# Expert weights of one fused layer kernel: the down matrices move from SyncE's DMA queue to ScalarE's

## The reference

```
logits = hf @ w_router + b_router             # 256 tokens, 32 experts, top 4 kept
gu  = xb @ w_gate_up[e] + b_gate_up[e]        # [rows,1024] @ [1024,2048]
g   = min(gu[:, :1024], 7);  u = clip(gu[:, 1024:], -7, 7)
y   = ((u + 1) * g * sigmoid(1.702 * g)) @ w_down[e] + b_down[e]   # [rows,1024] @ [1024,1024]
x  += weighted sum of y over the four experts of each token
```

## Time and profile before

| what | value |
|---|---|
| median of three runs | 1425.66 us |
| the profiled execution | 1425.22 us |
| its span | 1423.0 us |
| PE busy | 1337.5 us (94%) |
| ACT busy | 316.1 us (22%) |
| DVE busy | 479.2 us (34%) |
| DMA, whole span | 498.75 MB, mean 351 GB/s |

### The profile page before, as it was taken

The page is one execution under the profiler, slowest core; times in us unless marked ns, Lnnn a source line. Parts: engine busy times, 40 slices in busy tenths (PEclk is TensorE's granted clock), DMA queues, the critical chain, the costliest instruction groups (busy, mean ns, idle before and its releaser), DMA issues.

```text
span 1423.0 us, 16623 instructions
## 1 busy us (share of the span) xinstructions
PE 1337.5 (94%) x6794; PEld 712.5 (50%) x6794; DVE 479.2 (34%) x696; ACT 316.1 (22%) x416; POOL 36.2 (3%) x50
## 2 busy tenths in 40 slices
PE   8989999999999999999899999898999989999998
PEld 5758866334334333333333333333333336897996
DVE  3676665112112111211121111211112116775764
ACT  4254633011111110110111101111011114632531
POOL 2110100000000000000000000000000000000000
PEclk9999999999999999999999999999999999999999
DMA  9982397999999999999999999999999996355330
GB/s 326 387 323 89 107 380 322 418 428 428 428 428 428 428 429 428 429 428 427 429 429 428 428 429 428 427 429 429 428 429 429 428 408 207 120 183 192 125 120 30
DMA packets 76975, 498.75 MB, mean 351 GB/s; under 512 B 7095, under 2 KB 8586, under 8 KB 52362
## 3 DMA queue, kind: packets, MB, share of 16 engines
q1 hardware_dynamic: 75802, 496.06, 85.3%
q0 software_dynamic: 704, 2.10, 0.5%
q10 hardware_dynamic: 432, 0.07, 0.0%
HBM read 497.06 MB, written 1.05 MB: 350 GB/s over the span
## 4 chain that ended last, share of the span: by engine, by line
PE 60%; DMA 24%; DVE 6%; ACT 2%; issue 1%; POOL 0%; SPq 0%; DVEq 0%; ACTq 0%
PE ps L1765 31%; DMA ring<-in_w_gate_up_dram 21%; PE ps L1501 5%; PE ps L1503 5%; PE ps L1502 5%; PE ps L1759 3%; DMA arena<-in_w_gate_up_dram 2%; PE ps L1746 1%; PE ps L1830 1%; ACT arena L760 1%; PE ps L1522 1%; PE ps L1769 1%; PE ps L1523 1%; PE ps L1528 1%; DVE ring_low L891 1%
## 5 line engine op out<-in xcount | busy, mean ns | idle before, releaser
L1765 PE MATMUL ps<-ring,arena 128*64 128x512 f32 x2304 | 518.1, 600 | 33.1 <-DMA ring<-in_w_gate_up_dram 22.1
L1765 PEld LDWEIGHTS ps<-ring,arena 128*64 128x64 f32 x2304 | 159.4, 138 | 364.5 <-issue 300.3
L1765 PE MATMUL ps<-arena 128*64 128x512 f32 x768 | 175.2, 608 | 5.2 <-ACT arena L760 3.3
L1251 DVE TENSOR_SCALAR arena<-ps 128x512 f32<-128x512 f32 x32 | 22.1, 692 | 347.6 <-PE ps L1765 347.6
L753 ACT ACTIVATE arena<-arena 128x512 f32<-128x512 f32 x32 | 20.2, 630 | 498.6 <-DVE arena L1251 498.6
L1765 PEld LDWEIGHTS ps<-arena 128*64 128x64 f32 x768 | 53.7, 139 | 117.3 <-issue 102.2
L1503 PE MATMUL ps<-arena_highs,w_low 128*128 128x256 f32 x384 | 108.4, 282 | 0.0
L1210 DVE TENSOR_SCALAR esel<-const 128x128 fp32r<-128x128 f32 x49 | 12.6, 286 | 278.9 <-ACT arena L764 141.0
L764 ACT COPY arena<-ps 64x512 f32<-64x512 f32 x64 | 37.1, 580 | 239.6 <-PE ps L1765 239.2
L1230 DVE TENSOR_TENSOR X<-X,ps 128x1024 f32<-128x1024 f32 x34 | 41.4, 1218 | 124.2 <-PE ps L1759 124.2
L1501 PE MATMUL ps<-arena_highs,ring_highs 128*128 128x256 f32 x256 | 72.0, 281 | 2.3 <-DVE HT_r L1291 2.3
(11 more groups left out here) (284 smaller groups left out, 1591.9 us busy)
## 6 DMA issues: line engine op xcount, KB each, us to landing
ring<-in_w_gate_up_dram SPq DMA_DIRECT2D x96, 2048.0 KB, 31.2
ring<-in_w_down_dram SPq DMA_DIRECT2D x48, 2048.0 KB, 34.7
arena<-in_w_gate_up_dram SPq DMA_DIRECT2D x32, 2048.0 KB, 32.2
ring<-in_w_in_dram SPq DMA_DIRECT2D x38, 1024.0 KB, 7.2
arena<-in_w_down_dram SPq DMA_DIRECT2D x16, 2048.0 KB, 34.3
ring<-in_w_ada_dram SPq DMA_DIRECT2D x24, 1024.0 KB, 10.2
ring<-in_w_out_dram SPq DMA_DIRECT2D x12, 1024.0 KB, 7.4
ring<-in_w_ple_gate_dram SPq DMA_DIRECT2D x4, 1024.0 KB, 26.9
```

What stands on the lines that cost most here:

```text
L1251: V.tensor_scalar(glu, ps[:, 0, :], LIMIT, None, ALU.min).then_inc(s["g_ready"], 1)
L1765: last = T.matmul(ps[at:at + CAP, bank, :], lhsT, w(g), start=False, stop=stop)
```

## The change

A helper `load_down(eng, e, s)` holds the load of a down chunk, so that any engine can issue it. Chunks 4 and 5 (the downs of expert 0) are still asked for by SP ahead of the loop. All other down chunks are skipped in SP's list and asked for by ACT: after the copies of line 764 for expert n and after their `y_ready`, ACT asks for d0 and d1 of expert n+1, with no wait of their own. That they come after T(n) is what makes their bins free. ACT's loop is over four experts instead of two, the last four experts stand behind it, and a loop without loads follows for further rounds, which depend on the routing.

```
+        def load_down(eng, e, s):
+            src = dn_v[ds(e, 1), s % GROUPS - 4].rearrange("e p j n -> (e p) j n")
+            eng.dma_start(bin2(s).rearrange("p a (b n) -> p (a b) n", b=2), src).then_inc(ring2[s % BINS], 16)
...
                 else:
-                    src = dn_v[ds(e, 1), q - 4].rearrange("e p j n -> (e p) j n")
-                    sp.dma_start(two.rearrange("p a (b n) -> p (a b) n", b=2), src).then_inc(ring2[s % BINS], 16)
-
-            def quad(e, used):
+                    load_down(sp, e, s)
+
+            def quad(e, used, kinds=GROUPS):
                 for s in range(PER_QUAD):
-                    used(s)
-                    load(e + s // GROUPS, s)
+                    if s % GROUPS < kinds:
+                        used(s)
+                        load(e + s // GROUPS, s)
...
             for k in range(BINS, PER_QUAD):
-                sp.wait_ge(s["chunk_used2"], k - BINS + 1)
-                load(k // GROUPS, k)
+                if k % GROUPS < 4:
+                    sp.wait_ge(s["chunk_used2"], k - BINS + 1)
+                    load(k // GROUPS, k)
...
-            with act.Fori(0, extra * PAIRS + PAIRS) as i:
+            def pair_of_experts(i, loads):
                 for e in range(2):
...
                     last.then_inc(s["y_ready"], 1)
+                    loads(e)
+
+            def four_experts(i, expert, n):
+                for half in range(2):
+                    def loads(e):
+                        k = 2 * half + e + 1
+                        if k <= n:
+                            for q in (4, 5):
+                                load_down(act, expert + k, k * GROUPS + q)
+                    pair_of_experts(i * 2 + half, loads)
+
+            with act.Fori(0, QUADS - 1) as i:
+                four_experts(i, i * 4, 4)
+            four_experts(QUADS - 1, E - 4, 3)
+            with act.If(extra > 0):
+                with act.Fori(0, extra * PAIRS) as i:
+                    pair_of_experts(i + PAIRS, lambda e: None)
```

More of the change, by code:

```diff
@@ L516, in _ @@
             for k in range(BINS, PER_QUAD):
-                sp.wait_ge(s["chunk_used2"], k - BINS + 1)
-                load(k // GROUPS, k)
+                if k % GROUPS < 4:
+                    sp.wait_ge(s["chunk_used2"], k - BINS + 1)
+                    load(k // GROUPS, k)
             with sp.Fori(0, QUADS - 1) as i:
-                quad(i * 4 + 4, lambda k: sp.wait_ge(s["chunk_used2"], i * PER_QUAD + (PER_QUAD + k - BINS + 1)))
+                quad(i * 4 + 4, lambda k: sp.wait_ge(s["chunk_used2"], i * PER_QUAD + (PER_QUAD + k - BINS + 1)), 4)
             sp.wait_ge(s["routed"], 1)
```

## The result

The changed kernel took 1434.3 us (median of five runs, 1430.93 to 1437.53), the kernel before 1425.59 us beside it: a ratio of 1.0063, 95% interval 1.0044 to 1.0082, slower. The forecast was 1436.0 us. Measured once more later, the same kernel took 1433.48 against 1424.27 us, ratio 1.0072 (1.0058 to 1.0085). The profiled execution took 1434.3 us with a span of 1431.7 us, 8.7 us longer than before.

What follows compares the result with a forecast made beforehand. The prediction took the DMA engines, at 428 GB/s and 29.4 us an expert, to bound the loop, with PE close behind. It summed 5.9 (start) + 0 (steady loop) + 4.4 (end) = +10.3 us, 1436.0 us, range 1433 to 1443.

Steps and rivals of the forecast that it cites:

- Issuing: 62 issues move from SP's queue to ACT's, ahead of a sigmoid before which ACT idled 16.5 us: cost 0.
- Term 1, the gap: At the loop's start the DMA engines run dry before chunk 12, which waits for expert 0: +5.9 us.
- Term 2, the steady loop: Downs' request loop takes 28.2 us an expert at half rate, below the DMA engines' 29.4 us: cost 0.
- The margin: In the steady loop, the 1.2 us by which the downs' request loop stays under the DMA engines' 29.4 us.
- Term 3, the end: At the loop's end phase 3's loads run ahead of expert 31's last down and take 5.4 us: +4.4 us.
- the r of the prediction: Data of q3 still left to transfer when the next expert's downs are asked for, in us: 4.4.
- The rival of faster transfers: Two queues let each engine start its next packet sooner; at 437 GB/s 18 us less, 1418 us; chance 6%.
- that of a gap that doesn't count: The loop would end with PE, not with the DMA engines: no change, about 1426 us; chance 6%.
- The order of arrival: Engines serve requests as they come, phase 3's four half chunks ahead of the last downs: +12.7 us, 1438.4 us; chance 10%.
- The thin margin: Rival in the steady loop: the downs' request loop passes 29.4 us; at 45% of the rate +50 us, 1475 us; chance 12%.

Runs made afterwards that it cites:

- The run behind the copies: Changed kernel with ACT's two requests held back until its own copies of the result are done: 1433.48 against 1423.99 us for the kernel before, ratio 1.006.
- the run with eight and four: Changed kernel with the downs of experts 1 to 8 and 28 to 31 back on SP's queue: 1424.55 us, +0.3 us over the kernel before, ratio 1.0004.
- the run without the gap: Changed kernel with the downs of experts 1 to 8 back on SP's queue: 1426.96 us, +2.7 us over the kernel before, ratio 1.0025.
- the last four: Changed kernel with the downs of experts 28 to 31 back on SP's queue: 1429.2 us, +4.9 us over the kernel before, ratio 1.0042.
- Last downs back: Changed kernel with the downs of expert 31 asked for by SP again, behind its q3: 1433.72 us, +10.1 us over the kernel before, ratio 1.0067.
- a request one chunk later: Changed kernel with ACT's two requests held back until PE has used q0 of the next expert: 1553.04 us, +129 us over the kernel before, ratio 1.0907.

## Why the prediction was right

**Issuing: right.** 62 issues of some 0.35 us on ACT cost nothing that is seen: PE's waits for ACT's copy of line 765 (760 before) are 14.5 us in all, against 14.3. The step before them was wrong by 1.2 us: I put them behind ACT's two copies, and the trace has the first issue at 275.98, while the first copy runs from 275.82. The run behind the copies shows no difference in time from this.

**Term 1, the gap: right in place and size** (5.9 us forecast, 6.6 us in the windows, 6.5 us between two timed kernels). My reason named chunk 12's wait for expert 0, which is right for this kernel, but one expert later there is such a gap as well; the runs showed the general form.

**Term 2, the steady loop: right.** I had taken the halves of the rate from one row of a small load, and there was some luck in that. The queues shared 54 to 46, d1 landed 23.0 us after its request (I had 23.3), and the loop over the downs took 27.4 us, not 28.2. Two queues move 428 to 429 GB/s as one does, and with ACT at 19 experts the time is that of before. The margin was as thin as forecast: PE waited for downs six times, but the DMA engines stayed busy, and no loss by it is seen. The Trainium skill, "DMA: Bandwidth & Descriptors", section "Issuing engines are not separate DMA queues", says that starting DMAs on several engines only saves the time of issuing; the run with eight and four agrees at +0.3 us. The same page of the Trainium skill, section "Queues, rings and completion order", has the engines go round between queues by whole packets. Where both queues held rows of 16 KB that came to near halves. At 1162 to 1168 us ACT's queue held the last downs and SP's queue phase 3's loads in short pieces (packets, MB, share):

```profile
q10 hardware_dynamic: 113, 1.64, 64.5%
q1 hardware_dynamic: 264, 0.81, 33.9%
```

ACT's queue, with 14.5 KB a packet against 3.1, got two thirds of the time and twice the bytes, so the turns aren't of equal bytes. The counts, 113 to 264, aren't equal either, so they aren't turns of one packet each as the profile counts packets. How long a turn is, no run here settles.

**Term 3, the end: the size came near (4.4 us forecast), but partly by luck, as its mechanism was wrong.** What was lost beside the gap is 1.7 us in the profiled execution (8.7 less 6.6 and 0.4), 2.7 us in the run without the gap, and 4.3 us by the gain of the last four. The step that failed is that phase 3's loads ahead of the last down make the loss. They took less than I gave them: d1 of expert 31 landed 18.8 us behind its request, at 1168.9 us and not at 1172.0, and from the landing of q3 to then SP's queue had 39% of some 8.3 us, 3.3 us and not 5.4. And taking them out of the way, in "Last downs back", gained nothing. What decides is how late PE is at T(30): 11.8 us, of which 6.6 are the gap, 0.4 the start, and the remaining 4.8 about one chunk, d0, ahead of q3 of the same expert. I had seen that the downs delay q3 (the r of the prediction, 4.4 us; q3 of expert 30 came 14.5 us behind T(29), which gives 4.7), but had not carried this lateness to T(30) as a bound of its own. In the last expert 3.1 us come back, because PE hardly waits for transfers in it, only 0.3 us for q3. I had the 16.3 us behind q3 as fixed, and it was 15.1. That the order is what the last four experts gained back is shown by the runs; that it amounts to the one chunk is worked out from landing times and fits, but no run tests it alone.

**Sum.** I had forecast 10.3 us, and 8.7 and 9.2 us were measured. The rival of faster transfers fell with the rate of 428 GB/s, and that of a gap that doesn't count with the run of the first eight. The order of arrival fell at the end of the loop: a load of phase 3 of 1024 KB that SP had asked for ahead of ACT's request for d1 of expert 31, before 1149.8 us, landed 25.5 us later, and d1 landed 18.8 us behind its request at 1150.1. The thin margin cost nothing in this kernel, but a request one chunk later used it up.

## What to carry to other kernels

The loop here, bound by transfers, lost nothing by a second queue and gained nothing. What counted was when requests are made while the queue is shallow, and what lands ahead of what at the end. Ask whether the last data to arrive is that behind which the most work stands. Where two engines are within some per cent of each other, lateness is made up slowly, 1.9 us in 27.5 here, so an order must be put right several rounds before the end.

## What the runs showed that I had not expected

ACT issued a DMA at 275.98 us while its own earlier copy, 275.82 to 276.40, still ran. A request that needs the copy's result would have to wait for its semaphore, and one that doesn't came 1.2 us sooner here than program order suggests. And a short wait of TensorE can cost twice: behind one of 2.3 us a chunk took 5.35 us, in a stretch at 0.72 of the clock, instead of 3.65, though behind another of 3.5 us it took 3.65.
